# Retention heads written out and interlocked in a two-block model kernel

## The reference, cut to what matters

```python
def step(state, qkv):                      # retention_scan, one direction, per chunk
    qc, kc, vc = qkv
    scores = jnp.einsum('bhid,bhjd->bhij', qc, kc) * decay_in
    out = jnp.einsum('bhij,bhjv->bhiv', scores, vc) + jnp.einsum('bhid,bhdv->bhiv', qc, state) * decay_q
    state = state * decay_chunk + jnp.einsum('bhjd,bhjv->bhdv', kc * decay_k, vc)
    return state, out

def retention_bidir(q, k, v, log_g, s0_fwd, s0_bwd):
    o_f, s_f = retention_scan(q, k, v, log_g[0], s0_fwd, False)
    o_b, s_b = retention_scan(jnp.flip(q, 2), jnp.flip(k, 2), jnp.flip(v, 2), log_g[1], s0_bwd, True)
    return o_f + jnp.flip(o_b, 2), s_f, s_b

def retention_readout(o, g):
    b, h, n, dv = o.shape
    o = rms_norm(o).transpose(0, 2, 1, 3).reshape(b, n, h * dv)
    return jax.nn.silu(g) * o.astype(g.dtype)
```

## Time and profile before

| | us |
|---|---|
| median of three runs | 4649.26 |
| lowest, highest | 4647.08, 4651.5 |
| the profiled execution | 4654.9 |
| its span | 4653.1 |
| TensorE busy in the span | 4133.0 (89%) |
| VectorE, ScalarE, GpSimd busy | 1282.1, 1020.9, 463.7 |
| the granted clock of TensorE, mean | 0.947 of full |

### The profile page before, as it was taken

How to read it: one execution, slowest core, us unless ns; L and a number is a source line. 1 busy time by engine, 2 the same in 40 slices (tenths; PEclk the granted TensorE clock), 3 DMA queues, 4 the chain that set the end, 5 groups by cost and what they waited for, 6 DMA issues and landing times. The chain is left out here.

```text
span 4653.1 us, 96296 instructions
## 1 busy us (share of the span) xinstructions
PE 4133.0 (89%) x41717; PEld 2682.6 (58%) x41717; DVE 1282.1 (28%) x2323; ACT 1020.9 (22%) x2419; POOL 463.7 (10%) x663
## 2 busy tenths in 40 slices
PE   7898799986999979999978987989999989997995
PEld 2343346875444448888854443449888844444774
DVE  2424321122000230001033554225665520112002
ACT  2200100013000112222233332024444410011333
POOL 0010000000000000000010000005545400000112
PEclk8899899997999979999989999989999989998998
DMA  5361211101211139999971001100000031113998
GB/s 207 116 187 61 101 46 63 36 9 39 78 32 32 58 140 385 397 397 399 396 265 32 7 4 32 36 14 4 4 4 4 4 121 47 32 58 127 385 386 319
DMA packets 246294, 588.53 MB, mean 126 GB/s; under 512 B 36264, under 2 KB 153943, under 8 KB 226360
## 3 DMA queue, kind: packets, MB, share of 16 engines
q1 hardware_dynamic: 203087, 454.52, 26.8%
q0 software_dynamic: 26976, 103.32, 6.7%
q10 hardware_dynamic: 16010, 27.46, 1.6%
HBM read 514.20 MB, written 71.05 MB: 126 GB/s over the span
## 5 line engine op out<-in xcount | busy, mean ns | idle before, releaser
L1539 PE MATMUL experts_bank<-experts_uT,ex_wu 128*64 128x96 f32 x9216 | 391.1, 247 | 25.2 <-PE experts_bank L1525 18.6
L1539 PEld LDWEIGHTS experts_bank<-experts_uT,ex_wu 128*64 128x64 f32 x9216 | 384.8, 138 | 41.9 <-issue 41.9
L192 PE MATMUL vgproj_bank<-vg_w,mix_hT 128*128 128x256 f32 x1024 | 225.6, 383 | 11.0 <-DVEq L201 7.6
L1729 PE MATMUL taps_bank<-b2z_hT,taps_w 128*128 128x512 f32 x480 | 212.7, 602 | 22.5 <-DMA taps_w<-in_w_in 16.5
L1171 DVE TENSOR_TENSOR merge_pr<-merge_bank,merge_sg 128x512 f32<-128x512 f32 x64 | 44.3, 692 | 680.9 <-ACT merge_sg L1158 407.3
L1612 DVE TENSOR_TENSOR experts_hT<-experts_si,experts_bank 128x384 f32<-128x384 f32 (+1 forms) x68 | 31.3, 460 | 723.3 <-PE experts_bank L1539 723.3
L1144 PE MATMUL merge_bank<-b2z_hT,merge_w 128*128 128x512 f32 x512 | 222.3, 592 | 0.0
L1144 PE MATMUL merge_bank<-mix_hT,merge_w 128*128 128x512 f32 x512 | 222.3, 592 | 0.0
L192 PEld LDWEIGHTS vgproj_bank<-vg_w,mix_hT 128*128 128x128 f32 x1024 | 195.7, 192 | 41.4 <-DVEq L201 8.4
L1539 PE MATMUL experts_bank<-experts_uT,b2z_hT 128*64 128x96 f32 x4096 | 178.0, 248 | 27.7 <-DMA b2z_hT<-in_w 18.6
L1539 PEld LDWEIGHTS experts_bank<-experts_uT,b2z_hT 128*64 128x64 f32 x4096 | 172.6, 138 | 42.4 <-issue 42.4
(11 more groups left out here) (501 smaller groups left out, 6561.9 us busy)
## 6 DMA issues: line engine op xcount, KB each, us to landing
ex_wu<-in_expert_w SPq DMA_DIRECT2D x72, 2048.0 KB
mixed_T<-in_expert_w SPq DMA_DIRECT2D x36, 2048.0 KB, 23.8
b2z_hT<-in_w SPq DMA_DIRECT2D x64, 1024.0 KB
b2z_Z<-in_w SPq DMA_DIRECT2D x32, 1024.0 KB
keep_rows<-mix_hyT POOLq DMA_DIRECT2D x27, 768.0 KB, 4.7
keep_rows<-experts_yo ACTq DMA_DIRECT2D x68, 288.0 KB
mix_hT<-in_ada_w POOLq DMA_DIRECT2D x8, 2048.0 KB, 10.2
merge_w<-in_w_in SPq DMA_DIRECT2D x32, 512.0 KB, 5.8
```

Source lines behind the costliest of these rows:

```text
L192: last = pe.matmul(bk[t][:, 0:width], xT[:, k, t * P:(t + 1) * P], wt[:, s, k, :], start=(k == 0), stop=(k == KT - 1))
L1539: last = pe.matmul(bk[2 + j][c:c + 64, h * BT:(h + 1) * BT], wu[:, s, j, k, h * P + c:h * P + c + 64], uT[:, s, k, :], start=(k == 0), sto ...
L1729: last = pe.matmul(bk[s * 2 + h][:, :], wt[:, s, k, :], xT[:, k, h * HALF:(h + 1) * HALF], start=(k == 0), stop=(k == KT - 1))
```

## The change

- The four heads are written out (no loop, no address registers).
- GpSimd does nothing; `qr` is gone. TensorE and VectorE read `qk` itself. `qd` has two buffers, one for odd and one for even heads.
- TensorE: key turning and scores of the first head stand ahead of everything; those of head h+1 stand between the output products and the row turning of head h.
- The backward direction's updates and states come first. Its first four updates wait for 8 scaled keys in place of 16; the forward ones wait for all of the preceding head's stores.
- The output products of chunks 0 and 1 wait for the backward states and three forward ones; those of each later pair for two more.
- The row turning writes into banks 0 to 3, each pair of chunks over its own outputs, once both are normalised (`normed`).
- VectorE: masks of head h+1 stand behind the gating of head h, the scaled queries of head h+1 behind the states of head h.
- ScalarE: scaled keys of the first head come first, then Silu over the gates of all heads in one instruction; the scaled keys of head h+1 stand behind the root of head h, ahead of its stores, which are eight copies of 128x256 in place of four of 128x512.

The added side of the diff; the lines taken away stand in the listing above.

```diff
 
     NCH = SEQ // P
     with Mem(nc, "ret") as m:
...
+        qd = m.sb("qd", [P, 2, 2, SEQ])
         kn = m.sb("kn", [P, 2, NCH, P])
         on = m.sb("on", [P, NCH, RV])
         sc = m.sb("sc", [P, NCH, P])
         sq = m.sb("sq", [P, 2, RV])
         ss = m.sb("ss", [P, 3, NCH])
         bk = m.banks(8)
...
+        (gated, qdone, kturn, kscaled, scored, masked, upd, stated, outd, ssum, rstd, normed, turned, stored, inv) = m.sems(
+            "gated", "qdone", "kturn", "kscaled", "scored", "masked", "upd", "stated", "outd", "ssum", "rstd", "normed", "turned", "stored", "inv")
         b = m.block()
...
+        chunk = lambda c: slice(c * P, (c + 1) * P)
+        place = lambda n: slice(n * RV, (n + 1) * RV)
+        value = lambda h, c: v[:, c, place(h)]
+        update = lambda d, n: bk[4 * d + n // 2][:, place(n % 2)]
+        chunk_of = lambda d, n: n if d == 0 else NCH - 1 - n
+        state_at = {1: 0, 0: NCH}
 
         @b.tensor
         def _(pe):
...
+
+            def scores(h):
+
+                for c in (4, 5, 6, 7, 0, 1, 2, 3):
+                    pe.transpose(bk[6 + c // 4][:, chunk(c % 4)], qk[:, 4 + h, chunk(c)], K.ident[:, :]).then_inc(kturn, 1)
                 for c in range(NCH):
...
+                    pe.matmul(bk[4 + c // 4][:, chunk(c % 4)], qk[:, 4 + h, chunk(c)], qk[:, h, chunk(c)], start=True, stop=True).then_inc(scored, 1)
+
+            scores(0)
+            for h in range(RH):
+                pe.wait_ge(masked, 2 * h + 2)
+                for n in range(NCH - 1):
+                    if n in (0, 4):
+                        pe.wait_ge(kscaled, 16 * h + (8 if n == 0 else 16))
+                    pe.matmul(update(1, n), kn[:, 1, chunk_of(1, n), :], value(h, chunk_of(1, n)), start=True, stop=True).then_inc(upd, 1)
+                if h:
+                    pe.wait_ge(stored, 4 * h)
+                for n in range(NCH - 1):
+                    pe.matmul(update(0, n), kn[:, 0, n, :], value(h, n), start=True, stop=True).then_inc(upd, 1)
+                pe.wait_ge(qdone, 2 * h + 2)
                 for c in range(NCH):
...
+                    o = bk[c // 2][:, place(c % 2)]
+                    pe.wait_ge(stated, 16 * h + 8 + min(c // 2 * 2 + 3, 8))
+                    pe.matmul(o, sc[:, c, :], value(h, c), start=True, stop=False)
+                    pe.matmul(o, qd[:, h % 2, 0, chunk(c)], st[:, 0, c, :], start=False, stop=False)
+                    pe.matmul(o, qd[:, h % 2, 1, chunk(c)], st[:, 1, c, :], start=False, stop=True).then_inc(outd, 1)
+                if h + 1 < RH:
+                    scores(h + 1)
                 for c in range(NCH):
...
+                    pe.wait_ge(normed, NCH * h + c // 2 * 2 + 2)
                     for x in range(2):
...
+                        pe.transpose(bk[c // 2][:, chunk(c % 2 * 2 + x)], on[:, c, chunk(x)], K.ident[:, :]).then_inc(turned, 1)
 
         @b.vector
         def _(dve):
...
+
+            def queries(h):
+
                 for d in range(2):
...
+                    dve.tensor_tensor(qd[:, h % 2, d, :].rearrange("p (c n) -> p c n", n=P), qk[:, h, :].rearrange("p (c n) -> p c n", n=P),
+                                      R.DQ[:, h:h + 1, d, :].to_broadcast([P, NCH, P]), ALU.mult).then_inc(qdone, 1)
+
+            def masks(h):
+
                 for x in range(2):
...
+                    dve.wait_ge(scored, NCH * h + 4 * x + 4)
                     dve.tensor_tensor(sc[:, 4 * x:4 * x + 4, :], bk[4 + x][:, :].rearrange("p (c n) -> p c n", n=P),
...
+                                      R.DT[:, h:h + 1, :].to_broadcast([P, 4, P]), ALU.mult).then_inc(masked, 1)
+
+            masks(0)
+            queries(0)
+            for h in range(RH):
+                for d in (1, 0):
+                    first = chunk_of(d, 0)
+                    dve.tensor_copy(st[:, d, first, :], R.S0[:, d, h, :]).then_inc(stated, 1)
                     for n in range(NCH - 1):
...
+                        c, nx = chunk_of(d, n), chunk_of(d, n + 1)
+                        dve.wait_ge(stated, 16 * h + state_at[d] + n + 1)
+                        dve.wait_ge(upd, 14 * h + (7 if d == 0 else 0) + min(n // 2 * 2 + 2, NCH - 1))
+                        dve.scalar_tensor_tensor(st[:, d, nx, :], st[:, d, c, :], R.DC[:, d, h, 3:4], update(d, n), ALU.mult, ALU.add).then_inc(stated, 1)
+                if h + 1 < RH:
+                    queries(h + 1)
                 dve.wait_ge(rstd, h + 1)
                 dve.reciprocal(ss[:, 2, :], ss[:, 1, :]).then_inc(inv, 1)
                 dve.wait_ge(inv, h + 1)
...
+                dve.wait_ge(gated, 1)
+                if h:
+                    dve.wait_ge(turned, 16 * h)
                 for c in range(NCH):
...
+                    dve.scalar_tensor_tensor(on[:, c, :], bk[c // 2][:, place(c % 2)], ss[:, 2, c:c + 1], g[:, c, place(h)],
+                                             ALU.mult, ALU.mult).then_inc(normed, 1)
+                if h + 1 < RH:
+                    masks(h + 1)
 
         @b.scalar
         def _(act):
...
+
+            def keys(h):
+
+                for d in (1, 0):
+                    for n in range(NCH):
+                        c = chunk_of(d, n)
+                        act.wait_ge(kturn, NCH * h + (4 if c >= 4 else 8))
+                        act.activation(kn[:, d, c, :], bk[6 + c // 4][:, chunk(c % 4)], ACT.Copy, scale=R.DC[:, d, h, 0:1]).then_inc(kscaled, 1)
+
+            keys(0)
+            act.activation(g[:, :, :], g[:, :, :], ACT.Silu).then_inc(gated, 1)
+            for h in range(RH):
                 for c in range(NCH):
...
+                    act.wait_ge(outd, NCH * h + c // 2 * 2 + 2)
                     if c >= 2:
...
+                        act.wait_ge(ssum, NCH * h + c - 1)
+                    act.activation(sq[:, c % 2, :], bk[c // 2][:, place(c % 2)], ACT.Square, accum_out=ss[:, 0, c:c + 1]).then_inc(ssum, 1)
+                act.wait_ge(ssum, NCH * h + NCH)
                 act.activation(ss[:, 1, :], ss[:, 0, :], ACT.Sqrt, scale=1.0 / RV, bias=K.eps[:, 0:1]).then_inc(rstd, 1)
...
+                if h + 1 < RH:
+                    keys(h + 1)
+                for n in range(4):
+                    act.wait_ge(turned, 16 * h + 4 * n + 4)
+                    for x in range(2):
+                        last = act.activation(qk[:, h + 4 * x, place(n)].rearrange("p (c n) -> p c n", c=2),
+                                              bk[n][:, :].rearrange("p (c x n) -> p x c n", c=2, x=2)[:, x, :, :], ACT.Copy)
+                    last.then_inc(stored, 1)
 
 
 C = 512
```

More of the change, by code:

```diff
@@ L503, in _ @@
                     for x in range(2):
-                        pe.transpose(bk[4 + c // 4 + 2 * x][:, c % 4 * P:(c % 4 + 1) * P], on[:, c, x * P:(x + 1) * P],
-                                     K.ident[:, :]).then_inc(turned, 1)
+                        pe.transpose(bk[c // 2][:, chunk(c % 2 * 2 + x)], on[:, c, chunk(x)], K.ident[:, :]).then_inc(turned, 1)
         @b.vector
         def _(dve):
-            dve.sem_inc(normed, 1)
-            dve.sem_inc(qdone, 1)
-            with dve.Fori(0, RH) as h:
-                dve.wait_ge(taken, h * 2 + 2)
+            def queries(h):
@@ L539, in _ @@
+                if h + 1 < RH:
+                    masks(h + 1)
         @b.scalar
         def _(act):
-            act.sem_inc(stored, 1)
-            with act.Fori(0, RH) as h:
-                act.activation(g[:, :, bass.ds(h * RV, RV)], g[:, :, bass.ds(h * RV, RV)], ACT.Silu).then_inc(gated, 1)
-                for c in range(NCH):
-                    hold(act, kturn, h * 8 + (c // 4 * 4 + 4))
-                    for d in range(2):
-                        act.activation(kn[:, d, c, :], bk[6 + c // 4][:, c % 4 * P:(c % 4 + 1) * P], ACT.Copy,
-                                       scale=R.DC[:, d, bass.ds(h, 1), 0:1].rearrange("p a b -> p (a b)")).then_inc(kscaled, 1)
-                for c in range(NCH):
-                    act.wait_ge(outd, h * 8 + (c // 2 * 2 + 2))
+            def keys(h):
[4 more added lines that the diff above has]
+                        act.activation(kn[:, d, c, :], bk[6 + c // 4][:, chunk(c % 4)], ACT.Copy, scale=R.DC[:, d, h, 0:1]).then_inc(kscaled, 1)
@@ L555, in _ @@
-                act.wait_ge(ssum, h * 8 + 8)
+                        act.wait_ge(ssum, NCH * h + c - 1)
+                    act.activation(sq[:, c % 2, :], bk[c // 2][:, place(c % 2)], ACT.Square, accum_out=ss[:, 0, c:c + 1]).then_inc(ssum, 1)
+                act.wait_ge(ssum, NCH * h + NCH)
                 act.activation(ss[:, 1, :], ss[:, 0, :], ACT.Sqrt, scale=1.0 / RV, bias=K.eps[:, 0:1]).then_inc(rstd, 1)
-                for x in range(2):
-                    for y in range(2):
-                        hold(act, turned, h * 16 + (8 * y + 9))
-                        act.activation(qk[:, bass.ds(h + 4 * x, 1), y * HALF:(y + 1) * HALF].rearrange("p a n -> p (a n)"),
```

(3 more changed lines are left out.)

63 lines of the change are left out of this document (removed).

## The result

| | before | after |
|---|---|---|
| median, us | 4649.46 (4 runs) | 4591.16 (4 runs) |
| lowest, highest | 4647.08, 4651.5 | 4586.46, 4596.57 |
| the profiled execution, and its span | 4654.9, 4653.1 | 4586.46, 4584.3 |
| stage: last value product to last store | 161.4 | 98.6 |

The ratio of the runs is 0.9865, 95% interval 0.9851 to 0.9879: 56 to 69 us less. The forecast was 4595.3 in a range of 4586 to 4609. The stage, read from the trace, gave 62.8 us where the working had 54.0.

The account below looks back on a forecast made before the run. The stage was taken as bound by a serial chain over three engines. First head to 1011.7, three crossings 75.8 and tail 6.6 put the last store at 1094.1 for 1148.1, 54.0 us less: 4595.3, range 4586 to 4609.

Parts of the forecast that it names:

- First head: From first key turning at 988.45 to last output product at 1011.7, 5.9 us early, including 1.0 for low clock.
- Crossing: From one head's last output product to the next's: 23.85 us at full clock, 24.85 with 1.0 for clock falls.
- Masks, not keys, release the updates: At each crossing, the second mask, not scaled keys, starts the updates, 6.55 us after the last product, before 16.3.
- Stores in time: ScalarE's eight stores end 8.1 to 8.7 us after the last product, before forward updates due at 9.55.
- Sqrt's load: Sqrt's table load ahead of gating, 1.28 us, goes in every head but the first.
- one or two falls: Main forecast for TensorE's clock at crossings: 1.0 us charged per crossing, 54.0 us less in all; chance 0.50.
- the case of no fall: Rival: the clock never falls, last store at 1090.1, 58.0 us less, 4591; chance 0.15.
- a fall at every crossing: Rival: clock falls at each crossing and before the first outputs, 49.1 us less, 4600; chance 0.24.
- Low clock throughout: Rival: all updates and outputs at low clock, 2.7 us more, 4652; chance 0.05, shared with partial fetches.
- fetching of code: Rival: written-out heads' first instructions fetched from memory, 63 us slower in all, 4713; chance 0.01 at full price.
- Late stores: Rival: stores at 0.6 us each delay crossings by 0.9, 2.7 in all, 4598; counted within the clock cases.
- a gain above 60 us: Remaining case, not seen by the forecaster, such as more overlap at the state chain; chance 0.05.

Follow-up runs that it names:

- second experiment: Kernel before with heads written out, old order kept, and unread products filling TensorE's gaps: 4641.37 us (one run), stage 141.2 us.
- first experiment: Kernel before with its four heads written out and nothing else: 4648.08 us, ratio 0.9983 to the kernel before, stage 152.4 us.
- eighth experiment: Changed kernel with the first backward updates waiting for all 16 scaled keys in place of 8: 4596.03 us (one run), stage 98.8 us.
- fifth experiment: Changed kernel with ScalarE's scaled keys of the next head behind its stores: 4613.67 us (one run), stage 110.8 us.
- seventh experiment: Changed kernel with Silu in four pieces, one a head ahead of the squares: 4596.83 us (one run), stage 103.1 us.
- experiments 3: Changed kernel once more, as it is: 4596.82 us, ratio 0.9875 to the kernel before, stage 98.6 us.
- experiments 4: Changed kernel with next head's key turning and scores behind the row turning: 4604.18 us, ratio 0.9891 to the kernel before, stage 111.0 us.
- 6: Changed kernel with all output products waiting for all 16 states of the head: 4606.41 us (one run), stage 112.3 us.
- 9: Changed kernel, next head's masks after two gated chunks, backward updates before row turning, forward pairs awaiting only their own bank's store: 4595.99 us (one run), stage 98.2.
- 10: Kernel with early backward updates, plus the first head's scaled queries on GpSimd in place of VectorE: 4587.66 us, ratio 0.9865 to the kernel before, stage 95.5.

## Why the prediction was right, by its steps

**What bounds.** That the stage is a serial chain and that nothing behind it takes the gain back held: the stage gave 62.8 us, the span from the stage's start to the end 63.0 (68.8 - 5.8).

**First head.** Worked out 23.25 us from the first key turned to its last product; it took 1003.79 - 982.15 = 21.6. The 1.0 for a low stretch was not paid; handovers gave the rest. TensorE also began 0.5 us nearer to the last value product (1.25 in place of 1.75), which I had not counted.

**Crossing.** Gating began 1.48 us after the last product (worked out 1.7), updates 5.96 (6.55), backward states 7.2 (7.85), products 12.16 (13.35), next end 22.75 (23.85 at full clock, 24.85 with the allowance). All of the order was right, each handover a little too long. The largest unit that I had too large is that of the loop with its addresses from registers: from one direction's first step to the other's 4.28 us before, 1038.85 - 1035.03 = 3.82 after. The second experiment shows the same 3.82 (1034.87 - 1031.05) and the first the same steps, so this comes from writing out, since the order is the old one there. The sum had no term for the registers' going. The masks are another matter: two in 1.48 us before, 1.28 after, but in the first experiment each still takes 0.69 and the second waits for its scores. The 1.48 had such a wait in it; with all scores ready it goes. One small reading failed: the working has TensorE waiting for the third forward state, with its updates done 0.8 us earlier. In the trace it is at its updates (1036.92 + 3.19) until the products begin (1039.99) and waits for no state in the crossings.

**Masks, not keys, release the updates:** right, shown by the eighth experiment. **Stores in time:** right; in the second crossing they ended at 1032.96 + 2.42 = 1035.38, 7.6 us after the last product, 1.5 before the forward updates that wait for them could begin. (What the updates wait for in the fifth experiment is the keys, not the stores.)

**Sqrt's load:** 24.04 - 22.76 = 1.28 us between the first crossing and the third, and again in the seventh experiment.

**The clock.** The forecast had one or two falls as likeliest; the case of no fall, at 0.15, is what both profiles of the changed kernel show. In 12 crossings of this order of steps (after, and experiments 3, 7, 8) it never fell. No gap of TensorE in those crossings is over 1.03 us; the working had 1.1 us ahead of the updates, which is 0.54 in the trace. This is the term that was mis-sized: 4.0 us charged, 0 paid. With handovers (4.3) and the start (0.5) it makes the 8.8 us by which the stage came out shorter than the 107.4 (105.65 + 1.75) of the working. The rule of the Trainium skill (page "TensorE: Matmul & The Clock Gate", Part 4, that a transposition is not counted as busy in the same way) I had read as a fall at every crossing. It did not come, though the turning did; what went with a fall was a longer gap. With 0.5 us between row turning and updates the clock held; with 2.9 (the fifth) it fell each time; with the scores late, so that TensorE had nothing and then only turning behind its products, it fell in two of three. Whether transpositions count at all, these runs don't decide. Nor does the length of the gap settle it alone: behind gaps of 2.2 to 2.5 us the clock fell at some places and held at others (experiments 4, 6, 9 and 10), with the same code and the same gap. Small moves open such a gap, as in experiments 6 and 9, and lose the clock in some crossing. As far as these runs show, the changed kernel keeps the clock because no such gap is left in its crossings; its tail still has one of 2.4 us, and the clock held there in both profiles.

**Rivals.** Low clock throughout and fetching of code fell (the first experiment, and clock 1.00). Late stores fell. That the gain is the clock's rather than the order's, which was not among the rivals, is settled by the second experiment: of 62.8 us, 9.0 are the writing out with the clock that it brought, 11.2 what was still missing of the clock in the old order, 42.6 the new order with what goes along with it. Undone one at a time, with the clock that each costs, the place of the scores is worth 12.4 us of stage, that of the keys 12.2, the products released stepwise 13.7, the one Silu 4.5 and the updates released on half of the keys 0.2; these do not add up to a sum. GpSimd's copies are worth 2.6 us ahead of the first key turned (3.85 us after the last value product before, 1.27 after). The backward direction going first, the second buffer of `qd` and the banks of the row turning were not tested one by one.

**Sizes.** The whole came out at 58 us by medians against 54, and here luck had a part. The stage, which is what the working added up, gave 62.8: more than the 58.0 of its case of no fall, and in the case of a gain above 60 us, which had 0.05 and was said not to be seen. The 4.5 us between 62.8 and the 58.3 of the medians lie outside the stage, where the start alone varies by 9 us; with a stage of 62.8 and no such help the time would have been 4586.7, at the lower end of the range.

## What to carry to other kernels

Where the engines take turns, lay the crossing out from the end of one unit of work, count for each engine what it must have done before the next can begin, and put the independent work of the next unit (here key turning and scores) where TensorE would wait. Here it paid twice, since with the shorter gaps TensorE's clock stayed up; to tell the two apart, fill the gaps of the old order with products that nobody reads. When TensorE's busy time comes near the length of the crossing, little more is to be had: here 0.7 of the last 0.9 us a head. At that point look at TensorE's longest gap as well as at the sum, for a gap of 2.2 us in one crossing took back most of the gain in one of two profiles.

## What the hardware showed that was not expected

- More work was faster: with 160 MATMUL instructions in a crossing in place of 116, the old order's crossing fell from 37.6 to 34.9 us.
- The loop with its addresses from registers cost VectorE time at each handover: state steps of 0.55 us on average with, 0.51 without; from the copied first state to the first step 0.52 with, 0.33 without. Whether the addresses or the computed wait counts take it was not separated.
- The same gap of TensorE, in the same code, was followed by a low clock at one time and by a full one at another: 2.4 us ahead of the row turning (experiment 4), 2.5 us ahead of the products (6), 2.2 us ahead of the updates (9 and 10).
- The last value product, ahead of all that was edited, started anywhere from 979.2 to 988.5 us in the profiles of these kernels: 9 us of spread that belongs to no edit.
